# Six places for expert weights made seven for gate and up, with the split cross attention output moved out of their way

## What is computed

```python
def memory_cross_attention(h, m, w_cq, w_ck, w_cv, w_co):
    ...
    p = jax.nn.softmax(scores, axis=-1)
    o = jnp.einsum('bhsm,bmhd->bshd', p, v).reshape(b, s, X_HEADS * X_HEAD_DIM)
    return o @ w_co

for e in range(N_EXPERTS):                       # 32
    hid = jax.nn.silu(t @ w_exp_gate[e]) * (t @ w_exp_up[e])     # [., 1024] @ [1024, 256]
    out = out + combine[:, e:e + 1] * (hid @ w_exp_down[e])      # [., 256] @ [256, 1024]
```

## Time and profile before

| | us |
|---|---|
| median of 3 runs | 829.1 |
| lowest, highest | 828.96, 829.15 |
| the profiled execution | 829.2 |
| its span on the core | 827.4 |

### The profile page before, as it was taken

How to read it: one execution, slowest core, us unless ns; L and a number is a source line. 1 busy time by engine, 2 the same in 40 slices (tenths; PEclk the granted TensorE clock), 3 DMA queues, 4 the chain that set the end, 5 groups by cost and what they waited for, 6 DMA issues and landing times.

```text
span 827.4 us, 14485 instructions
## 1 busy us (share of the span) xinstructions
PE 775.1 (94%) x5739; PEld 623.0 (75%) x5739; DVE 343.8 (42%) x767; ACT 239.2 (29%) x417; POOL 312.3 (38%) x354
## 2 busy tenths in 40 slices
PE   5999999999999999999999999998999999988785
PEld 5987788888988877788888887866777777756651
DVE  6466651474575484325512624372222221121126
ACT  5344242112221458632222445331111111110012
POOL 3774434542242244143542454334333333322111
PEclk9999999999999999999999999999999999999998
DMA  9956832402202232446478255679999999999976
GB/s 250 167 108 119 266 66 55 98 2 52 51 1 53 51 102 52 94 102 187 81 157 229 70 173 183 254 282 343 388 388 388 390 387 383 392 386 381 390 299 250
DMA packets 74347, 166.95 MB, mean 202 GB/s; under 512 B 18838, under 2 KB 46310, under 8 KB 66344
## 3 DMA queue, kind: packets, MB, share of 16 engines
q1 hardware_dynamic: 65856, 150.66, 57.7%
q0 software_dynamic: 5392, 9.61, 3.5%
q10 hardware_dynamic: 3032, 5.74, 2.2%
HBM read 157.31 MB, written 16.97 MB: 211 GB/s over the span
## 4 chain that ended last, share of the span: by engine, by line
PE 64%; DMA 25%; DVE 4%; POOL 2%; issue 2%; ACT 2%; SPq 1%; DVEq 0%; POOLq 0%; ACTq 0%
DMA arena<-in_w_exp_up 23%; PE bank L1067 15%; PE bank L1074 13%; PE bank L1076 13%; PE bank L1075 13%; PE bank L1424 2%; DMA arena<-y_half 1%; PE bank L1434 1%; PE bank L1115 1%; PE bank L1225 1%; PE bank L1167 1%; POOL w_low L889 1%; PE bank L1279 1%; POOL xres L927 1%; PE bank L1411 1%
## 5 line engine op out<-in xcount | busy, mean ns | idle before, releaser
L869 POOL TENSOR_TENSOR ring_low<-ring,w_high 128x512 fp32r<-128x512 f32 (+1 forms) x64 | 83.6, 1306 | 124.7 <-ACT w_high L1516 120.7
L1074 PE MATMUL bank<-h_hi,w_high 128*128 128x512 f32 x296 | 122.1, 412 | 0.9 <-ACT arena L1630 0.9
L1075 PE MATMUL bank<-h_lo,w_high 128*128 128x512 f32 x296 | 115.8, 391 | 0.0
L1424 PEld LDWEIGHTS bank<-arena,hT 128*64 128x64 f32 x1728 | 96.6, 136 | 24.1 <-issue 12.5
L1424 PE MATMUL bank<-arena,hT 128*64 128x128 f32 x1728 | 100.7, 274 | 8.2 <-DMA arena<-in_w_exp_up 6.1
L869 POOL TENSOR_TENSOR w_low<-ring,w_high 128x512 fp32r<-128x512 f32 x56 | 75.1, 1341 | 59.9 <-ACT w_high L1516 55.8
L2142 DVE SCALAR_TENSOR_TENSOR rt<-rt,bank 128x128 f32<-128x128 f32 x32 | 9.2, 288 | 175.2 <-ACT rt L1733 175.2
L1516 ACT ACTIVATE w_high<-ring 128x2048 fp32r<-128x2048 f32 (+1 forms) x32 | 58.9, 1839 | 57.1 <-PE bank L1076 37.2
L1074 PEld LDWEIGHTS bank<-h_hi,w_high 128*128 128x128 f32 x296 | 55.7, 188 | 15.2 <-issue 3.5
L1076 PE MATMUL bank<-h_hi,ring_low 128*128 128x512 f32 x168 | 66.1, 393 | 0.0
L1075 PEld LDWEIGHTS bank<-h_lo,w_high 128*128 128x128 f32 x296 | 55.7, 188 | 9.5
(11 more groups left out here) (325 smaller groups left out, 1368.7 us busy)
## 6 DMA issues: line engine op xcount, KB each, us to landing
arena<-in_w_exp_gate SPq DMA_DIRECT2D x27, 1024.0 KB
arena<-in_w_exp_up SPq DMA_DIRECT2D x27, 1024.0 KB
arena<-in_w_exp_down SPq DMA_DIRECT2D x27, 1024.0 KB
ring<-in_w_in SPq DMA_DIRECT2D x33, 512.0 KB, 6.7
ring<-in_w_exp_gate SPq DMA_DIRECT2D x5, 1024.0 KB
ring<-in_w_exp_up SPq DMA_DIRECT2D x5, 1024.0 KB
ring<-in_w_exp_down SPq DMA_DIRECT2D x5, 1024.0 KB
xres<-in_x SPq DMA_DIRECT2D x8, 512.0 KB, 7.3
```

The lines of the kernel that those rows point to most:

```text
L869: after(pool.tensor_tensor(low, full, high, ALU.subtract), w_lo if kk == KD - 2 else step["pool"])
L1074: pe.matmul(o, l_hi, r_hi, start=(n == 0), stop=False)
L1075: pe.matmul(o, l_hi, r_lo, start=False, stop=False)
L1424: ins = pe.matmul(bank[CAP * half:CAP * half + CAP, 1, P * n:P * n + P], xgT[:, x, kk, :], w[:, kk, P * half:P * half + P], start=(kk == 0 ...
```

## The change

- Gate and up weights get seven places (GATES = 7) instead of six: expert e's go to place e % 7, where the seventh is the last 2048 words of the arena (gate) and xres[:, 2:4], the residual rows of tiles 2 and 3 (up). Down weights keep six places.
- For that, tile 3's residual is put into PSUM before the expert loop: new jobs k3 0 and k3 1 between g0 3 and ls, in banks 2 and 3; ls goes to bank 5. KEEP_AT and keep_residual go.
- The cross attention's split output is written elsewhere: the low part of tile t to the second half of probability row t (over hT), the high part to its first half, for tile 3 to the second half of rows[:, 0].
- SP asks for all of expert 3 and for down of expert 2 after cq 3; gate of expert 6 behind expert 4, and up of expert 6 after k3 1.
- In the loop SP asks for gate and up of e, then for down of e - 1; each step waits for gu_done and down_done of expert e - 7. Down of expert 31 comes last.
- y_rows moves to words 22528 to 30719 of the arena; gain_out is asked for after the down matmuls of expert 28.

```diff
-KEEP_AT = {26: 3}
+GATES = UNROLL + 1
...
-    jobs += [("g0", 0), ("g0", 1), ("pos", 3), ("g0", 2), ("g0", 3), ("ls",), ("gt",), ("most",)]
+    jobs += [("g0", 0), ("g0", 1), ("pos", 3), ("g0", 2), ("g0", 3), ("k3", 0), ("k3", 1), ("ls",), ("gt",), ("most",)]
...
-LATE_BANKS = {"g0": 0, "gt": 0, "ls": 3, "most": 4, "kr": 6}
+LATE_BANKS = {"g0": 0, "gt": 0, "k3": 2, "ls": 5, "most": 4, "kr": 6}
+KEPT = ("kr", "k3")
...
+        x_row_parts = y_hi[:, :, :].rearrange("p k t -> p (k t)")
+        out_homes = [x_row_parts[:, D * t:D * t + 512] for t in range(NT - 1)] + [rows_high[:, 0, 512:D]]
+        out_hi = [home.rearrange("p (k l) -> p k l", k=4) for home in out_homes]
+        out_lo = [x_row_parts[:, D * t + 512:D * t + D].rearrange("p (k l) -> p k l", k=4) for t in range(NT)]
...
-            first = 2 * EW + (2 * t + j) * D
+            first = (UNROLL - 2) * EW - 2 * D + (2 * t + j) * D
...
+        def expert_parts(e):
+
+            def home(b):
+                return arena[:, b * EW:(b + 1) * EW] if b < UNROLL - 1 else ring[:, :, :].rearrange("p r w -> p (r w)")
+
+            n = e % GATES
+            if n < UNROLL:
+                gate, up = home(n)[:, 0:KD * FE], home(n)[:, KD * FE:2 * KD * FE]
+            else:
+                gate, up = arena[:, arena_words - KD * FE:arena_words], xres[:, 2:NT, :].rearrange("p t d -> p (t d)")
...
             job_done(sp, ("cq", X_HEADS - 1))
-            load_part(3, 0)
-            load_part(3, 2)
+            for i in range(3):
+                load_part(3, i)
+            load_part(2, 2)
...
             job_done(sp, ("co", NT - 1, 1))
-            load_part(2, 2)
-            load_part(3, 1)
             sp.wait_ge(hrow_ready, NT)
             for i in range(3):
                 load_part(4, i)
...
+            def load_down(e):
+                sp.wait_ge(down_done, e + 1 - UNROLL)
+                sp.dma_start(expert_parts(e)[2], expert_sources(e)[2]).then_inc(down_loaded[e % UNROLL], 16)
+
+            load_gate(GATES - 1)
+            job_done(sp, ("k3", 1))
+            load_up(GATES - 1)
+            for e in range(GATES, EXPERTS):
+                sp.wait_ge(w_loaded[(e - 2) % UNROLL], 32 * ((e - 2) // UNROLL) + 32)
                 sp.sem_inc(loading, 1)
...
+                sp.wait_ge(gu_done, e + 1 - GATES)
+                load_gate(e)
+                load_up(e)
+                load_down(e - 1)
+            load_down(LAST_EXPERT)
...
+            sp.wait_ge(down_done, EXPERTS - 3)
             sp.dma_start(gain_out, norm_final_g.rearrange("(o d) -> o d", o=1).to_broadcast([P, D])).then_inc(gains_in, 16)
-            sp.wait_ge(down_done, EXPERTS - 4)
...
-                    return split_sums(o, [(h_parts(kk, slice(t * P, (t + 1) * P)), w_parts(c0, kk, 0, 512, 4)) for kk in range(4)])
+                    return split_sums(o, [(out_parts(kk, t), w_parts(c0, kk, 0, 512, 4)) for kk in range(4)])
...
-                if k == "kr":
-                    job_empty(pe, ("co", 2, job[1]))
-                    return pe.matmul(o, ident, xres[:, 2, 512 * job[1]:512 * job[1] + 512], start=True, stop=False, skip_group_check=True)
+                if k in KEPT:
+                    t = 2 + KEPT.index(k)
+                    job_empty(pe, ("co", t, job[1]))
+                    return pe.matmul(o, ident, xres[:, t, 512 * job[1]:512 * job[1] + 512], start=True, stop=False, skip_group_check=True)
...
-                    copy(h_hi[:, 0:4, c * P:(c + 1) * P], oh4, h_hi_ready["ox"])
+                    copy(out_hi[c], oh4, h_hi_ready["ox"])
...
-                    s = (slice(0, P), slice(0, 4), slice(c * P, (c + 1) * P))
-                    after(tt(h_lo[s], oh4, h_hi[s].bitcast(F32), ALU.subtract), e)
+                    after(tt(out_lo[c], oh4, out_hi[c].bitcast(F32), ALU.subtract), e)
```

More of the change, by code:

```diff
@@ L216, in emptied_by @@
         return "act"
-    if job[0] in PARTIAL or job[0] == "kr":
+    if job[0] in PARTIAL or job[0] in KEPT:
         return None
@@ L318, in program @@
         elif job[0] in LATE_BANKS:
-            bank_index[job] = LATE_BANKS[job[0]] + (job[1] if job[0] == "kr" else 0)
+            bank_index[job] = LATE_BANKS[job[0]] + (job[1] if job[0] in KEPT else 0)
         else:
@@ L347, in program @@
         hT = sb("hT", [P, KD, T])
+        with nc.sbuf_tensor("rows_high", [P, 2, D], F32R) as rows_high:
+            pass
         rows = sb("rows", [P, 2, D])
@@ L732, in chunk_source @@
             return w[0, :, c0:c0 + width].rearrange("(k p) c -> p k c", p=P)[lo:lo + HALF]
[L734 to L739, removed]
+        def expert_parts(e):
[6 more added lines that the diff above has]
+                gate, up = arena[:, arena_words - KD * FE:arena_words], xres[:, 2:NT, :].rearrange("p t d -> p (t d)")
+            return [gate.rearrange("p (k f) -> p k f", k=KD), up.rearrange("p (k f) -> p k f", k=KD),
+                    home(e % UNROLL)[:, 2 * KD * FE:EW].rearrange("p (k n) -> p k n", k=2)]
         def expert_sources(e):
@@ L812, in _, with load_gate, load_up @@
                 load_part(4, i)
-            def load_expert(i, b):
-                parts, sources = expert_parts(b), expert_sources(i * UNROLL + b)
-                sp.wait_ge(w_loaded[(b - 2) % UNROLL], i * 32 + (32 if b >= 2 else 0))
-                sp.sem_inc(loading, 1)
[L819 to L829, removed]
+            def load_gate(e):
+                sp.dma_start(expert_parts(e)[0], expert_sources(e)[0]).then_inc(w_loaded[e % UNROLL], 16)
+            def load_up(e):
+                sp.dma_start(expert_parts(e)[1], expert_sources(e)[1]).then_inc(w_loaded[e % UNROLL], 16)
+            def load_down(e):
[6 more added lines that the diff above has]
+                sp.wait_ge(w_loaded[(e - 2) % UNROLL], 32 * ((e - 2) // UNROLL) + 32)
+                sp.sem_inc(loading, 1)
+                sp.wait_ge(gu_done, e + 1 - GATES)
[3 more added lines that the diff above has]
+            load_down(LAST_EXPERT)
             most = sp.value_load(most_i[0:1, :], min_val=0, max_val=T)
@@ L1085, in y_parts, with out_parts @@
                 return y_hi[:, kk, :], y_lo[:, kk, :]
+            def out_parts(kk, t):
+                return out_hi[t][:, kk, :], out_lo[t][:, kk, :]
             def h_parts(kk, columns=slice(0, T)):
@@ L1396, in _ @@
             for n, job in enumerate(jobs):
-                if before_in_bank[job] and before_in_bank[job][0] not in PARTIAL + ("kr",):
+                if before_in_bank[job] and before_in_bank[job][0] not in PARTIAL + KEPT:
                     job_empty(pe, before_in_bank[job])
@@ L1416, in turn_rows, with gate_up @@
                 turn(b, turned)
-            def gate_up(b, x, s):
-                gate, up, _ = expert_parts(b)
+            def gate_up(e, x, s):
+                gate, up, _ = expert_parts(e)
                 for kk in range(KD):
@@ L1441, in expert @@
                 pe.wait_ge(turned_sb, e1)
-                gate_up(b, b % 2, gu_done)
+                gate_up(e1 - 1, b % 2, gu_done)
                 if not turn_last:
@@ L1452, in expert @@
                     turn_next()
-                if e1 in KEEP_AT:
-                    keep_residual(KEEP_AT[e1])
-            def keep_residual(t):
-                for half in range(2):
-                    pe.matmul(sum_banks(t)[:, half, :], ident, xres[:, t, 512 * half:512 * half + 512], start=True, stop=False, skip_group_check=True)
             pe.sem_inc(turning, 1)
```

## The result

| | before | after |
|---|---|---|
| median of 20 runs | 829.18 us | 830.46 us |
| lowest to highest | 828.45 to 830.71 | 828.91 to 832.12 |
| profiled execution | 829.2 | 829.85 |
| its span | 827.4 | 828.0 |

The ratio is 1.0017, with a 95% interval of 1.0011 to 1.0023: slower by 0.1 to 0.2%, within the 0.2% that I had set as the bound of "the same". The forecast was 829.7. The profiled execution of the changed kernel is the fourth fastest of its 20, so its trace can account for 0.6 us of span; the median's 1.3 us are not traced in full.

What follows compares the result with a forecast made beforehand. TensorE leads until 727, then the expert weight stream sets the pace, followed by expert 30 and the tail. Lead 2.0 us against 2.6 taken back by the order gives +0.6: 829.7 us, range 825.5 to 831.8 (own range 827.7 to 830.9).

Steps and rivals of the forecast that it cites:

- the same: Whole kernel: measured time within 0.2% (1.7 us) of no change, 827.4 to 830.8; chance 0.53.
- Sum: Whole kernel: 829.2 us for the profiled run plus 0.6 gives 829.8; median 0.1 below, so 829.7.
- Two early parts: Down 2 and up 3 asked for at 499 instead of 546: the weight stream gains 0.8 us.
- Seventh place: Expert 6's gate and up asked for earlier: idle DMA time at 562 to 572 closes, 1.0 + 0.2 us.
- Lead 2.0 us: Weight stream in the expert stage: runs 0.8 + 1.0 + 0.2 us further ahead than before.
- rival 3: Stream lead under 1 us, or first gathers delaying expert 1 over 3 us: 831.3; chance 0.22 together with rival 4, early requests not early.
- The order takes back 2.6 us: End of the stream: down 30 becomes the 95th part instead of the 93rd, costing 797.5 - 794.94 = 2.6 us.
- Which part is awaited last: Before expert 30's down matmuls: down 30, the 95th part, lands last at 795.5; the other condition is met at 794.6.
- The first wait for weights: Late expert stage: TensorE first waits near expert 25, in front of the down matmuls, on in_w_exp_down.
- k3: 1.9 us: Tile 3's residual matmuls before the expert loop: expert 0 comes 1.9 us later, which TensorE has to spare.
- a new wait before expert 10: Early expert stage: a new wait there was named as a sign of the forecast being wrong; no size given.
- The tail, unchanged: From expert 30's down matmuls to the end: 32.5 us, including the scatter's 4.06, with no change counted in the sum.

Runs made afterwards that it cites:

- early_only: The kernel before with only the split output's new homes and down 2 and up 3 asked for early; 1.0006 of before.
- seventh_alone: The changed kernel with down 2 and up 3 asked for at 546 again, old order from expert 22, residual jobs ahead of pos 3; 0.9982 of before.
- old_order_late: The changed kernel, but from expert 22 on gate, up and down of one expert are asked for together again; 0.9987 of before.
- down_one_later: The kernel before with only the new order of requests, from expert 22 on; 1.0018 of before.
- k3_in_the_gap: The changed kernel with tile 3's two residual jobs moved ahead of pos 3, where TensorE waits for VectorE; 1.0008 of before.
- after_again: The changed kernel itself, nothing altered, timed again on another chip; 1.0007 of before.
- short_fill: The changed kernel with four small matmuls between transpose and down wait, for experts 26 to 29; 1.0014 of before.
- old_order_k3_gap: The changed kernel with the old request order from expert 22 on and tile 3's residual jobs ahead of pos 3; 0.9984 of before.
- old_order_k3_again: The changed kernel with old request order from expert 22 and tile 3's residual jobs ahead of pos 3, timed on another chip; 0.9977 of before.
- early_and_gains: The kernel before with split output's new homes, down 2 and up 3 asked for early, and final gains asked for at 546; 0.9995 of before.
- fill_before_down: The changed kernel with six small matmuls between transpose and down wait, for experts 25 to 30; 1.0045 of before.

## Why the prediction was right, step by step

- **Sum.** +0.6 us was forecast, for the profiled execution; its span grew by 0.6, the median by 1.3 (0.17%). The time was in the forecast's own range, and the likeliest case, "the same", is the one that came. That the profiled sum fits so closely is in part luck: the terms below show a smaller lead, a dearer order, a slower clock and a shorter tail, which about cancel.
- **Two early parts: 0.8 us.** Right, by early_only's one trace (788.68 against 789.45) and by the idle 546 to 552. Too small to be measured in the times.
- **Seventh place: the hole at 562 closes.** Right, share 1.01. Its worth of 1.2 us isn't borne out by the end of the stream: seventh_alone's expert 30 starts 0.2 us sooner than before.
- **Lead 2.0 us.** SP's requests give it: it asks for expert 22 when expert 20's up weights have landed, at 700.12 before and 694.89 after; in the new order these are one part (3.0 us) nearer the front, so the lead is 5.2 - 3.0 = 2.2 us. At the end it is less: down 29, the 92nd part, is awaited until 788.2 to 788.3, where the 92nd part before landed at 789.41, 1.1 to 1.2 us; and in old_order_late expert 30 starts 0.9 us sooner than before. So 2.0 us was too much for the end. A lead under 1 us is the condition of rival 3, and it isn't excluded: the changed kernel lies between the forecast and that rival. In 720 to 784 the changed kernel moves 382 GB/s, before 385. Why, is open: with the new order 382 (changed) and 387 (down_one_later) occur, with the old one 382 (seventh_alone) and 387 (old_order_late).
- **The order takes back 2.6 us.** Right in kind, and the best measured term: 1.7 to 2.6 us in the time between kernels that differ in the order alone, and 1.5 us in down_one_later, where the shorter tail is already taken off. The forecast's 2.6 was for the start of expert 30's down matmuls, and there the order costs between 1.8 us (k3_in_the_gap, 796.03, against 794.2 to 794.3) and 5.3 us (after_again, 799.30, against old_order_late, 794.00), the larger ones with slow groups of matmuls on the path.
- **Which part is awaited last.** The prediction had the 95th part (down 30) at 795.5 as the last condition. In the changed kernel's trace it wasn't: expert 29's down part and the slow matmuls behind it set 797.16. Where it was last, it landed at 796.0 (k3_in_the_gap) and 795.48 (short_fill), so the landing was well placed, within 0.5 us; what was missing is the clock, which pushed the other condition from 788.3 + 7.2 = 795.5 to 797.2. The first wait for weights came at expert 24, where expert 25 was forecast, and at the place forecast, in front of the down matmuls.
- **k3: 1.9 us.** Expert 0 came 2.06 us later (561.31, before by the same row 559.25). Expert 1 was forecast at 570.6 and came at 572.38, for its gathered rows weren't there (1.39 us of waiting), the gathers in a full stream of which rival 3 speaks. That is a new wait before expert 10, which the prediction had named as a sign of being wrong, though a wait for rows and not for weights. In this profile the stream didn't suffer (share 1.02 in 572 to 604); in three of the experiments' profiles it did, by 0.4 to 0.6 us, so the margin that I had given as 3 us was thinner: I had reckoned with a late request, not with a clock that falls while TensorE waits.
- **The tail, unchanged.** Wrong: 1.7 us shorter. I had taken the scatter's 4.06 us for fixed; it was 2.5 in the changed kernel, most likely because less of the stream was left. This and the clock are the two terms that the sum lacked, -1.7 and +1.7, and by luck they cancelled in the profiled execution.

On the ring order I had cited the Trainium skill ("DMA: Bandwidth & Descriptors", Queues, rings and completion order). The traces agree as far as they go. The parts were awaited in the order of their places: the 92nd until 789.41 and the 95th until about 797.5 before, the 92nd until 788.2 in the changed kernel and the 95th until 796.0 in k3_in_the_gap. And the engines don't end together: the share in 794 to 798 is 0.65 in the changed kernel and 0.09 behind it. Which engine was last, and whether it had idled at 562, no view here shows, so the slowest engine's part in the small lead stays open.

The fastest version by its median is all of the change, but with down asked for beside gate and up of the same expert from 22 on, and k3 in TensorE's wait (old_order_k3_gap and old_order_k3_again, the same kernel): 0.9984 and 0.9977 of before. seventh_alone (0.9982) and old_order_late (0.9987) are not told apart from it.

## What to carry to other kernels

In a stage paced by one saturated queue, count each transfer's place in the queue and ask which consumer is the last one to wait: an order that asks for a later step's data first costs places at the end, where no reserve is left, so the order near the end is to be chosen by itself. Whether it helps earlier, while there is a reserve, was not settled here. Room for data earlier was worth only the idle time that it filled, not its bytes: two parts moved forward gave 0.8 us, because the stretch that they left went idle. And look at what else runs at the end on the same engines: here the scatter took 4.1 us before and 2.5 in the changed kernel, where less of the stream was left.

## What the runs showed of the hardware that I had not expected

The granted clock fell to 0.50, the lower of its levels, in the middle of the expert stage. In the changed kernel it fell behind waits of 1.06 and 2.90 us that stood between TensorE's single transpose and the down matmuls. Down matmuls then took 3.28 to 3.68 instead of 1.94 us, and gate and up matmuls behind such a group 4.1 to 5.0 instead of 3.77. But it didn't fall behind each such wait (2.16 and 1.12 us in the same trace, with 1.94 us behind them), and it isn't bound to that place or to the new order. Waits in front of the 64 gate and up matmuls left it at 1.00 up to 1.95 us in the kernel before, yet behind 2.02 us in early_and_gains they took 5.43 us, and in old_order_k3_gap the window 760 to 770 had a mean of 0.83 behind 2.26 us. At expert 1 it fell behind a wait of 1.90 us for the gathered rows in after_again (mean 0.79 in 572 to 580) and behind 1.34 in fill_before_down, and stayed at 1.00 behind 1.39 in the changed kernel. So these traces don't tell which wait brings it down. With the waits filled by matmuls of no use (fill_before_down) the clock stayed at 1.00 from 740 to 798.
